# Two triangular products per head split into row halves, and head sums as 64 by 64 tiles, in a hybrid RWKV-7 and retention step

## The reference

```python
def _rwkv7_step(S, inp):
    r, w, k, v, a, b = inp
    sa = jnp.einsum('bhvk,bhk->bhv', S, a)
    S = S * w[:, :, None, :] + sa[..., None] * b[:, :, None, :] + v[..., None] * k[:, :, None, :]
    y = jnp.einsum('bhvk,bhk->bhv', S, r)
    return S, y
```

## Time and profile before

| | |
|---|---|
| median of 3 runs | 4492.41 us (4488.85 to 4496.94) |
| the profiled execution's own time | 4495.93 us |
| its span in the trace | 4494.1 us, 86761 instructions |
| granted TensorE clock, mean | 0.97 |
| TensorE (PE) | 4180.5 us busy, 93% |
| weight loads (PEld) | 3701.4 us, 82% |
| VectorE (DVE) | 1967.4 us, 44% |
| ScalarE (ACT) | 1390.6 us, 31% |
| GpSimd (POOL) | 288.7 us, 6% |

### The profile page before, as it was taken

How to read it: one execution, slowest core, us unless ns; L and a number is a source line. 1 busy time by engine, 2 the same in 40 slices (tenths; PEclk the granted TensorE clock), 3 DMA queues, 4 the chain that set the end, 5 groups by cost and what they waited for, 6 DMA issues and landing times.

```text
span 4494.1 us, 86761 instructions
## 1 busy us (share of the span) xinstructions
PE 4180.5 (93%) x37496; PEld 3701.4 (82%) x37496; DVE 1967.4 (44%) x3000; ACT 1390.6 (31%) x2152; POOL 288.7 (6%) x464
## 2 busy tenths in 40 slices
PE   6999999999889988999979999999998899879996
PEld 5888889988866676999968888899887666869996
DVE  3434444444345544333354344444433455454443
ACT  4333333333222223222233333333332223132222
POOL 1000000000011011000100000000000110000000
PEclk9999999999999998999989999999999999989998
DMA  5122221222256564343321122212222565412221
GB/s 183 58 61 67 64 63 60 63 62 71 95 191 204 179 208 142 120 123 110 112 71 58 59 63 65 66 61 61 63 67 99 197 204 176 141 30 75 75 74 53
DMA packets 477319, 448.86 MB, mean 100 GB/s; under 512 B 18846, under 2 KB 409048, under 8 KB 476064
## 3 DMA queue, kind: packets, MB, share of 16 engines
q1 hardware_dynamic: 417712, 253.05, 18.5%
q0 software_dynamic: 41840, 157.01, 10.8%
q10 hardware_dynamic: 17408, 33.56, 2.0%
HBM read 345.79 MB, written 97.76 MB: 99 GB/s over the span
## 4 chain that ended last, share of the span: by engine, by line
PE 83%; DVE 7%; DMA 4%; ACT 3%; issue 2%; POOL 0%; ACTq 0%; DVEq 0%; SPq 0%; POOLq 0%
PE ps L721 82%; DVE scr L1880 3%; PE ps L725 1%; ACT scr L1351 1%; DMA w_raw<-in_w_branch_a_dram 1%; DMA scr<-in_ada_w_dram 1%; ACT w_hi L1364 1%; DVE scr L1882 1%; DVE w_lo L1893 1%; DVE h_lo L1880 1%; DVE scr L1952 1%; DVE lw L1880 1%; DVE acc L1880 0%; DMA scr<-in_state_ret_dram 0%; DMA out_dram<-scr 0%
## 5 line engine op out<-in xcount | busy, mean ns | idle before, releaser
L721 PE MATMUL ps<-h_hi,w_hi 128*128 128x320 f32 x4544 | 1105.7, 325 | 111.5 <-DVEq L1888 70.1
L721 PE MATMUL ps<-h_lo,w_hi 128*128 128x320 f32 x4544 | 1043.2, 311 | 0.0
L721 PE MATMUL ps<-h_hi,w_lo 128*128 128x320 f32 x4544 | 1042.0, 311 | 0.0
L721 PEld LDWEIGHTS ps<-h_hi,w_hi 128*128 128x128 f32 x4544 | 750.0, 190 | 200.1 <-issue 175.5
L721 PE MATMUL ps<-scr 64*64 64x64 f32 (+10 forms) x13248 | 808.5, 250 | 11.7 <-ACTq L1476 11.7
L721 PEld LDWEIGHTS ps<-h_lo,w_hi 128*128 128x128 f32 x4544 | 767.7, 190 | 0.0
L721 PEld LDWEIGHTS ps<-h_hi,w_lo 128*128 128x128 f32 x4544 | 767.1, 190 | 0.0
L721 PEld LDWEIGHTS ps<-scr 64*64 64x64 f32 (+4 forms) x13248 | 590.4, 141 | 209.9 <-issue 182.6
L1364 ACT ACTIVATE w_hi<-w_raw 128x1024 fp32r<-128x1024 f32 (+1 forms) x468 | 410.7, 878 | 808.7 <-PE ps L721 611.7
L1893 DVE TENSOR_TENSOR w_lo<-w_raw,w_hi 128x1024 fp32r<-128x1024 f32 (+1 forms) x468 | 469.5, 1003 | 359.7 <-ACT w_hi L1364 340.4
L1351 ACT ACTIVATE scr<-ps 128x512 f32<-128x512 f32 (+8 forms) x724 | 343.4, 474 | 763.9 <-PE ps L721 539.2
(11 more groups left out here) (151 smaller groups left out, 3131.4 us busy)
## 6 DMA issues: line engine op xcount, KB each, us to landing
w_raw<-in_w_in_dram SPq DMA_DIRECT2D x180, 512.0 KB, 3.7
scratch_z<-scr SPq DMA_DIRECT2D x128, 320.0 KB, 2.2
scr<-in_ada_w_dram POOLq DMA_DIRECT2D x40, 1024.0 KB, 5.9
scr<-in_state_ret_dram POOLq DMA_DIRECT2D x64, 512.0 KB, 4.9
out_dram<-scr ACTq DMA_DIRECT2D x64, 512.0 KB, 3.0
w_raw<-in_w_ffn_up_dram SPq DMA_DIRECT2D x64, 512.0 KB, 4.0
w_raw<-in_w_ffn_down_dram SPq DMA_DIRECT2D x128, 256.0 KB, 2.7
scr<-scratch_z POOLq DMA_DIRECT2D x24, 1280.0 KB, 8.8
```

The costliest lines, as they stand in the source:

```text
L721: return pe.matmul(out, lhsT, rhs, start=start, stop=stop, skip_group_check=True)
```

## The change

On TensorE's side alone, three things:
- `triangular` issues each of the ten products of the z and of the uw call as two. The first has the weights' upper row half (64 rows, 128 columns) and the moving operand's upper half, and writes all 128 output partitions. The second has the lower row half and only columns 64 to 127 (64 by 64), and adds to output partitions 64 to 127. The zero quarter is in neither. The second product of m is issued behind the first product of m + 2.
- the `start` flag is set for the first product of a bank alone (m = 0 and 8 for z, m < 2 for uw), and the second products accumulate;
- `head_totals` takes the place of `channel_sums` with `bones`: per half of the tokens one product for each head, with a 64 by 64 tile of ones as weights.

```diff
-            def channel_sums(mat, src, n, bank):
-                for hf in range(2):
-                    for i in range(n):
-                        last = mm(ps[:, bank + hf, 0:HALF], mat, src[:, i, HALF * hf:HALF * hf + HALF], i == 0, i == n - 1)
-                return last
...
+            def triangular(out, lhsT, rhs, start):
+
+
+                for m in range(2 * NBLK + 2):
+                    if m < 2 * NBLK:
+                        mm(out(m), lhsT[0:64, m], rhs(m)[0:64], start(m), False)
+                    if m >= 2:
+                        last = mm(out(m - 2)[64:128], lhsT[64:128, m - 2, 64:128], rhs(m - 2)[64:128], False, True)
+                return last
+
+            def head_totals(src):
+
+                for hf in range(2):
+                    for q in range(2):
+                        last = mm(ps[half(q), 5 + hf, 0:HALF], ones[half(q), half(q)], src[half(q), HALF * hf:HALF * hf + HALF])
+                return last
...
-                done(channel_sums(bones, t1[:, None, :], 1, 5), "pe_pr", n, "bs")
+                done(head_totals(t1), "pe_pr", n, "bs")
...
-                done(channel_sums(bones, yb[:, None, :], 1, 5), "pe_gn", n, "gn1")
+                done(head_totals(yb), "pe_gn", n, "gn1")
...
-                for m in range(2 * NBLK):
-                    last = mm(flat(5, 64 * m, 64), AKT[:, m], TOKB[:, 4 * (m // 2) + 3, half(m % 2)])
+                last = triangular(lambda m: flat(5, 64 * m, 64), AKT, lambda m: TOKB[:, 4 * (m // 2) + 3, half(m % 2)], lambda m: m in (0, 8))
                 M(last, "pe_in", "z")
...
-                for m in range(2 * NBLK):
-                    b, q = m // 2, m % 2
-                    mm(ps[:, 2 + q, 64 * b:64 * b + 64], XTF[:, m], Z_[:, m], b == 0, True)
+                triangular(lambda m: ps[:, 2 + m % 2, 64 * (m // 2):64 * (m // 2) + 64], XTF, lambda m: Z_[:, m], lambda m: m < 2)
```

## The result

The changed kernel takes 4696.3 us (median of 4 runs, 4692.8 to 4698.4), the kernel before 4490.9 in the same sittings: ratio 1.0456, 95% interval 1.0444 to 1.0469, which is 205 us slower. The forecast was slower, 4603 us, range 4545 to 4665: right in sign, the time outside the range. The profiled execution has a span of 4695.0 us.

What follows compares the result with a forecast made beforehand. TensorE's issue order in the head pairs was taken as the bound: +112 us for the z and uw calls and -1 for the head sums on 4495.9 gave 4607, by the median 4603 us, range 4545 to 4665.

Steps and rivals of the forecast that it cites:

- What bounds the kernel: In the head pairs TensorE's issue order is the time; a microsecond more or less in it counts in full.
- The sum for a triangular call: z and uw calls: 5.8 us against 2.22 and 2.26, taken as 3.5 more each, +112 us over 32 calls.
- The group prices: TensorE time per product group: lone two-record upper half 0.37 us, lone lower half 0.20 + 0.06.
- The decisive row: Where a 64*128 group meets a 64*64 one: changing tile shape drains TensorE, 0.2 us, 48 such changes counted in the trace.
- The 10% case: Rival for z and uw calls: independent row halves pay no shape change, +0.4 us a call, 4504 us; chance 10%.
- the case at half price: Rival for z and uw calls: a change waits only for its own row half, +56 us, 4548; chance 8%.
- The clause that the quarter left out saves nothing: z and uw calls: upper halves still load 128 columns ten times at 0.11 us per record.
- The head sums: gn1 and bs sums: row halves side by side, 1.07 us each as before; -1 us in all, between -4 and +34.
- The gn1 gain: Sums over the outputs between 64*64 groups: two tile changes fewer, 0.3 us saved at each of 14, 4.2 us.
- With bs: Sums over the channels, 14 between fillers and uw: one tile change more, 0.15 us each, +2.1 us.
- The step that failed: Granted clock stays 1.00 in the pairs; rival that it falls behind calls, 1 to 2 us each, +32 to +64, chance 14%.

Runs made afterwards that it cites:

- the upper halves alone: Against the changed kernel with the earlier head sums: each z and uw call issues only its ten upper-row products, lower ones left out; 4505.8 us, ratio 1.0026.
- The run with the upper halves twice: Against the changed kernel with the earlier head sums: each z and uw call issues its ten upper-row products two times, no lower ones; 4637.9 us, ratio 1.0326.
- the version with a filler unit inside: Against the changed kernel with the earlier head sums: one unit of 12 filler records moved into the middle of each call; 4664.3 us, ratio 1.0379.
- The version with two groups: Against the changed kernel with the earlier head sums: all ten upper halves first, then all ten lower, one tile change inside a call; 4588.2 us, ratio 1.0224.
- the one with four: Against the changed kernel with the earlier head sums: five upper, five lower, five upper, five lower halves, three tile changes per call; 4585.0 us, ratio 1.0216.

## Why the prediction was wrong in size

- **What bounds the kernel**: right. TensorE's issue order in the pairs is the time; nothing absorbed the longer calls.
- **The sum for a triangular call**: right. Forecast 3.5 us more per call; the uw call takes 5.61 undisturbed, and the least disturbed z call 5.72 (the clock is down for its last 0.28 us), against 2.27 and 2.22: 3.4 more, at most 109 us in all where 112 stood. The group prices read from the earlier trace rows hold to 0.01 us for lone halves that the kernel before never issued.
- **The decisive row**: right, and now shown: between two versions that differ in the tile's columns alone lie 3.0 us per call and 195 us in all, the clock's share with them. The 48 changes with 0.20 are those behind 64 moving columns; the trace before has 28 more, behind 320 columns, with 0.36. The 10% case that halves which share no row pay nothing is refuted, and with it the case at half price. The clause that the quarter left out saves nothing is shown by the upper halves alone, 2.37 us.
- **The head sums**: right, -1 forecast, 1.0006 measured. The rule of the Trainium skill, TensorEngine Tiling (Array Packing), Restrictions and Gotchas, that different row tiles cannot access one PSUM bank at the same time, does not bind where the halves write different partitions of a bank: the sum takes 1.08 us and not 2.14. The gn1 gain of 0.3 us came. With bs it is 1.46 us from the last filler record to the uw call in place of 1.22, 0.24 more, where 0.15 and the change into the call stood.
- **The step that failed** is the one of the forecast that left the clock at 1.00 and gave its fall 14%, at 1 to 2 us per call. It fell at every one of the 32 calls, inside 30 of them. With 205 measured and 109 from the calls at full clock, the fall costs 96 us, 3.0 us per call: 33 inside the calls (142 - 109) and 63 behind them. The difference of time at the lower level, 479 - 270 = 209 us, fits that: at half pace it costs 105 at most. So the case was real and too cheap, 3.0 us against 1 to 2, and the rest of the forecast stood beside it: 4603 + 96 is 4699, measured 4696.
- Why it was underrated: I weighed the share of time in which columns stream, 2.1 us in 5.8, against retention stretches with long waits, and took the pairs' steady 1.00 as a margin. The run with the upper halves twice shows that the clock falls also in a stream without any wait, when it uses 64 of the rows.

## What to carry to other kernels

Splitting these products by rows did not pay in any form: 2.65 us per call in place of 2.24 even in one shape with the halves side by side, and each change of shape cost 0.14 us more. Leaving zeros out saved nothing, because loads and changes, not multiplications, were the price. Only the gn1 sums, whose neighbours have the same shape, gained, 0.3 us each, and by less than can be measured in the whole. Price a small product by the group it stands in, from first start to first start of the next group. And add to any edit that leaves TensorE with smaller tiles the question what the granted clock will do: read it in the windows around the edited calls, since two thirds of that loss stood in the products behind them and a third in the calls themselves.

## What was not expected of the hardware

- A gapless stream of 40 records in 64*128 tiles of one row half for 4.6 us had the clock fall to its lower level in 20 of 32 calls; the same stream in 128*128 tiles, 4.5 us, in none. With the halves in turn, one shape, 2.65 us, it fell in none either, but neither did it in 2.37 us of one row half, so that call is too short to say more.
- A shorter stretch can be enough: in the version with a filler unit inside, 2.9 us of mixed shapes were followed by fillers at 0.54 us per pair of records instead of 0.29. With upper halves once, 2.4 us, there was no such fall. What exactly separates these is open.
- The version with two groups and the one with four cost the whole kernel the same, though the calls differ by 0.28 us x 32 = 9 us. Up to 35 us lie between runs of one of these kernels, which hides it; that falls come or stay away from run to run would explain this, and is not shown.
